# Moving x's rows and the rope tables' inputs behind more of the first weights, and masking the band by memsets on VectorE

## The reference, cut to what matters

```
h = rms_norm(x, mixer_norm)                      # x: (1, 256, 2048)
qkv = h @ w_qkv                                  # 2048 x 3072: 5 chunks of 512 columns with k and v in one
q, k = rope(rms_norm(q)), rope(rms_norm(k))      # cos and sin of positions * inv_freq
x = x + softmax(window(q k) with sinks) v @ w_o
x = x + (silu(h @ w_gate) * (h @ w_up)) @ w_down
...
# chunk_band_attention, 16 heads of 128:
s = q k^T * 128**-0.5 + bias[head, clip(i - j)]  # keys j of later chunks than i's are not in the band
p = softmax(s);  o = p v
```

## Time and profile before

| | us |
|---|---|
| median of 3 runs (lowest, highest) | 2476.63 (2476.08, 2476.88) |
| the profiled execution's own time | 2477.34 |
| its span | 2475.6 |
| PE busy | 2437.5 (98%) |
| DVE busy | 1734.6 (70%) |
| ACT busy | 1159.6 (47%) |
| mean DMA rate | 234 GB/s |
| granted TensorE clock, mean | 0.995 |

### The profile page before, as it was taken

The page is one execution under the profiler, slowest core; times in us unless marked ns, Lnnn a source line. Parts: engine busy times, 40 slices in busy tenths (PEclk is TensorE's granted clock), DMA queues, the critical chain, the costliest instruction groups (busy, mean ns, idle before and its releaser), DMA issues.

```text
span 2475.6 us, 30363 instructions
## 1 busy us (share of the span) xinstructions
PE 2437.5 (98%) x11143; PEld 1990.0 (80%) x11143; DVE 1734.6 (70%) x2394; ACT 1159.6 (47%) x1547; POOL 44.7 (2%) x64
## 2 busy tenths in 40 slices
PE   8999999999999999999999999999999999999997
PEld 6777888888888888788888888888888778888886
DVE  6785777777777776677678667677676576666655
ACT  5565544434443444544444434444444454455553
POOL 1110000000000000000000000000000000000000
PEclk9999999999999999999999999999999999999999
DMA  7434788888888887477777787777776457776653
GB/s 267 138 120 149 253 287 289 304 292 294 290 285 300 291 291 244 137 229 238 239 230 235 243 261 243 240 229 233 246 227 223 144 182 243 248 234 219 215 189 120
DMA packets 161827, 578.13 MB, mean 234 GB/s; under 512 B 18288, under 2 KB 20592, under 8 KB 161680
## 3 DMA queue, kind: packets, MB, share of 16 engines
q1 hardware_dynamic: 160432, 572.64, 70.3%
q0 software_dynamic: 1104, 3.28, 0.5%
q10 hardware_dynamic: 144, 0.26, 0.0%
HBM read 574.01 MB, written 2.10 MB: 233 GB/s over the span
## 4 chain that ended last, share of the span: by engine, by line
PE 92%; DVE 3%; ACT 2%; issue 1%; DMA 1%; SPq 0%; POOL 0%; DVEq 0%; ACTq 0%
PE PS L928 29%; PE PS L930 29%; PE PS L929 29%; PE PS L562 2%; DVE WL L1874 1%; ACT WH L1285 1%; DMA X<-in_x 0%; ACT SQ L963 0%; DVE AR L1394 0%; PE PS L662 0%; PE PS L635 0%; DMA ZG<-in_crow 0%; PE PS L833 0%; PE PS L758 0%; PE PS L778 0%
## 5 line engine op out<-in xcount | busy, mean ns | idle before, releaser
L1874 DVE TENSOR_TENSOR WL<-W,WH 128x1024 fp32r<-128x1024 f32 x816 | 993.6, 1223 | 563.9 <-ACT WH L1285 560.7
L1285 ACT ACTIVATE WH<-W 128x1024 fp32r<-128x1024 f32 x816 | 859.5, 1060 | 950.0 <-PE PS L930 941.5
L928 PE MATMUL PS<-WH,XTH 128*128 128x512 f32 x2144 | 858.5, 400 | 12.0 <-DVE WL L1874 4.7
L930 PE MATMUL PS<-WH,XTL 128*128 128x512 f32 x2144 | 838.3, 391 | 0.0
L929 PE MATMUL PS<-WL,XTH 128*128 128x512 f32 x2144 | 837.0, 390 | 0.0
L928 PEld LDWEIGHTS PS<-WH,XTH 128*128 128x128 f32 x2144 | 403.6, 188 | 103.5 <-issue 18.3
L930 PEld LDWEIGHTS PS<-WH,XTL 128*128 128x128 f32 x2144 | 403.5, 188 | 86.1
L929 PEld LDWEIGHTS PS<-WL,XTH 128*128 128x128 f32 x2144 | 404.1, 188 | 83.1 <-issue 3.8
L928 PE MATMUL PS<-WH,YTH 128*128 128x512 f32 x1120 | 442.1, 395 | 7.6 <-DVE YTL L1407 4.4
L930 PE MATMUL PS<-WH,YTL 128*128 128x512 f32 x1120 | 436.9, 390 | 0.0
L929 PE MATMUL PS<-WL,YTH 128*128 128x512 f32 x1120 | 436.6, 390 | 0.0
(11 more groups left out here) (267 smaller groups left out, 1161.8 us busy)
## 6 DMA issues: line engine op xcount, KB each, us to landing
W<-in_vec SPq DMA_DIRECT2D x192, 512.0 KB, 4.5
W<-in_avoz SPq DMA_DIRECT2D x192, 512.0 KB, 4.5
W<-in_wg SPq DMA_DIRECT2D x88, 512.0 KB, 4.6
W<-in_wu SPq DMA_DIRECT2D x88, 512.0 KB, 4.7
W<-in_wd SPq DMA_DIRECT2D x88, 512.0 KB, 4.7
W<-in_gate SPq DMA_DIRECT2D x64, 512.0 KB, 4.5
W<-in_aqk SPq DMA_DIRECT2D x64, 512.0 KB, 4.7
W<-in_aout SPq DMA_DIRECT2D x64, 512.0 KB, 4.4
```

What stands on the lines that cost most here:

```text
L928: e.matmul(p, x, WH[:, g % NH, j], start=first, stop=False)
L930: i = e.matmul(p, y, WH[:, g % NH, j], start=False, stop=last)
L1285: e.activation(WH[:, n % NH], W[:, i % NW], ACT.Copy).then_inc(s_hi, 1)
L1874: e.tensor_tensor(l, src, h.bitcast(F32), ALU.subtract).then_inc(s_lo, 1)
```

## The change

Five edits. (1) `square_in(0)` stays at the end of chunk 1, `square_in(1)` to `(3)` move to after slots 9, 11 and 12, and `stats(0)` from after slot 9 to after slot 13; X's pieces are issued ahead of tiles 10 to 17 and no longer 6 to 13. (2) Rows, positions and columns are issued after tile 4 and no longer after tile 1, and `rotary` starts one slot later. (3) `kv` is spread to fit (ticks counted from slot 8, two a slot): DVE reaches the factor's wait at tick 13 and no longer 6, `KD` is made at ticks 15 and 17 (9 and 13 before), PE transposes it at ticks 17 and 19 (12 and 14 before), ACT copies at 18 and 20. (4) The first rope of q waits for `s_kd` 2, DVE's own `KD`, and no longer for PE's transposes of it. (5) The mask matmul and `mband` go; DVE writes -1e30 into two blocks of 64 x 64 of the scaled scores with two memsets, and then waits for them before the maximum.

```diff
-    after[1].append(("start", "rotary"))
-    after[7] = [("square_in", 3)]
-    for c, k in enumerate((3, 5, 6)):
-        after[k].append(("square_in", c))
+    after[2].append(("start", "rotary"))
+    after[7] = [("square_in", 0)]
...
-        yield from chunk("X", 0, after={1: [("stats", 0)]} if g == 0 else {})
+        yield from chunk("X", 0, after={1: [("square_in", 1)], 3: [("square_in", 2)], 4: [("square_in", 3)],
+                                             5: [("stats", 0)]} if g == 0 else {})
...
             def kv(par, g):                       # PE
-                yield from ticks(11)
+                yield from ticks(16)
...
-                    e.matmul(b[:, 0:384], idb[:], mband[:], start=True, stop=False)
-                    e.matmul(b[:, 0:128], Q4[:, hh, 0:128], KT[:, h, 0:128], start=False, stop=False)
+                    e.matmul(b[:, 0:128], Q4[:, hh, 0:128], KT[:, h, 0:128], start=True, stop=False)
...
-                yield from ticks(8)               # ACT kv
+                yield from ticks(13)
...
-                yield                             # DVE kv
+                yield from ticks(8)
                 w.wait_ge(s_rst, 1)
...
-                yield from ticks(3)
+                yield from ticks(2)
...
-                    yield from ticks(4)
+                    yield from ticks(2)
...
-                        w.wait_ge(*filled(("kd", 1)))
+                        w.wait_ge(s_kd, 2)
...
                     w.wait_ge(s_bs, n + 1)
+                    for c in (64, 320):
+                        step(e.memset(s[0:64, c:c + 64], NEG))
+                    settle()
...
-            for c in (0, 256):                    # POOL
-                e.memset(mband[0:64, c + 64:c + 128], NEG).then_inc(s_const, 1)
...
-                if NW <= i < NW + 8:              # SP
-                    q = i - NW
+                if 10 <= i < 18:
+                    q = i - 10
...
-                if i == 1:
+                if i == 4:
                     e.dma_start(rows, A["rows"].to_broadcast([128, NROW])).then_inc(s_rows, 16)
                     e.dma_start(posi, A["pos"]).then_inc(s_pos, 16)
                     e.dma_start(cols[:, 32:NCOL], A["cols"][:, 32:NCOL]).then_inc(s_cols, 16)
```

More of the change, by code:

```diff
@@ L343 @@
 NORM_R = {0: 0, 1: 1, 2: 2, 3: 4}
-N_CONST = 13
+N_CONST = 10
 TWO_PI = 2.0 * np.pi
@@ L386, in build @@
         mrow = sb("mrow", [128, 256], BF16)
-        mband = sb("mband", [128, 384], BF16)
         mcT = sb("mcT", [128, 128], BF16)
@@ L1291, in scalar_program @@
             e.dma_start(xs(0), A["xt"][0]).then_inc(s_x[0], 16)
-            w.wait_ge(s_const, 6)
+            w.wait_ge(s_const, 5)
             e.activation(spare, nhalf[:, 0:4], ACT.Copy).then_inc(s_sc, 1)
@@ L1951, in gpsimd_program @@
             w = Waits(e)
-            for t, v in ((ident[:], 0.0), (onesf, 1.0), (mrow[:], 0.0), (mband[:], 0.0), (mcT[:], 0.0),
+            for t, v in ((ident[:], 0.0), (onesf, 1.0), (mrow[:], 0.0), (mcT[:], 0.0),
                          (nhalf[:], -0.5)):
                 e.memset(t, v).then_inc(s_const, 1)
-            w.wait_ge(s_const, 6)
+            w.wait_ge(s_const, 5)
             def select(ap, op, fill, pattern, cm):
@@ L1964, in gpsimd_program @@
             select(mcT[:], ALU.is_ge, NEG, [[1, 128]], -1).then_inc(s_const, 1)
-            for c in (0, 256):
-                e.memset(mband[0:64, c + 64:c + 128], NEG).then_inc(s_const, 1)
-            w.wait_ge(s_const, 12)
+            w.wait_ge(s_const, 9)
             e.tensor_copy(idb[:], ident[:]).then_inc(s_const, 1)
```

## The result

The changed kernel takes 2464.94 us (median of 5 runs, 2463.60 to 2465.74), the kernel before 2476.63 (5 runs, 2474.74 to 2478.77): ratio 0.9954, 95% interval 0.9943 to 0.9964, 11.7 us less. Measured again (run c3) it took 2466.05 against 2475.65, ratio 0.9959 (0.9947 to 0.9972), 9.6 us less.

The account below looks back on a forecast made before the run. PE was taken as the bound nearly everywhere, with much idle time only in the first stage. Terms: 8.1 + 1.7 + 2.7 - 0.5 = 12.0 us saved, forecast median 2464.6 us, range 2462.0 to 2469.5.

Parts of the forecast that it names:

- The start: Slots 2 to 8: slot 8 begins at 33.4 and not 41.54, 8.1 us saved, plus 1.7 from the slow stretch.
- The slow stretch of slots 8 and 9: At the start: half-clock matmuls after 2.38 us idle would go, since that gap goes, 1.7 us saved.
- The 2.65 us for the second tables: On DVE before slot 6: time from the second tables' start to the XTL behind them, taken from the earlier trace.
- kv: Spreading kv makes WL of slot 19 late on DVE, so PE waits: 0.5 us lost, bounds 0 and 2.5.
- the slower rival: Attention: DVE enters q's ropes over some 2 us later, WL late in four groups, 16.4 us lost, 2481 us; 3%.
- the sign of being wrong that I had set: Attention: PE idle beyond 2 us between 66 and 130 us would show the prediction wrong.
- The band: Band, 2190 to 2400 us: PE loses 16 mask matmuls of 0.17 us, 2.7 us saved, between 1.1 and 2.9.
- It costs nothing: Band: DVE's memsets and wait, 0.33 us a head, hide in its 36.5 us idle; without that cover 5.3 us.
- its own sign: Band: PE waiting there would show the prediction wrong; PE idle in the band was to stay 0.
- the lower row that I used: Band: POOL's rows of the same 64 x 64 block, 0.142 us, stood in for each memset of DVE.
- Half clock: Start or attention: a remaining gap or second late WL brings a paid slow stretch; saving 8 to 10.5, 2467.5 us; 20%.
- the central 12.0: Whole kernel: the likeliest saving, 12.0 us, giving a median of 2464.6 us; 62% for 2463 to 2466.5.

Follow-up runs that it names:

- c3: The changed kernel again, unaltered, beside the others on one chip: 2466.05 us.
- b1: The changed kernel with X's pieces issued ahead of tiles 6 to 13 again, squares left late: 2464.75 us, one execution.
- b2: The changed kernel with the tables as before: inputs issued after tile 1, rotary started after slot 1: 2464.20 us, one execution.
- a4: The changed kernel with rows, positions and columns issued after tile 1 again, rotary still one slot later: 2465.11 us, one execution.
- c2: The changed kernel with the tables' inputs issued after tile 3 and not 4: 2462.56 us, one execution.
- b4: The changed kernel with each of ACT's sines taken one tick later: 2462.80 us, one execution.
- b3: The changed kernel with the first rope of q waiting for PE's transposes of the second KD again: 2467.89 us, one execution.
- a3: The changed kernel without the memsets and the wait behind them, so the band is not masked: 2463.73 us, one execution.
- a1: The changed kernel with the mask matmul, mband and constants put back and the memsets taken out: 2466.74 us, ratio 0.9964 to the kernel before.

## Why the prediction was right, point by point

**The start, 9.8 us forecast, 10.1 measured.** The chain worked out for slots 2 to 8 was met slot by slot: 13.2, 15.9, 20.75, 23.5, 27.75, 30.65 and 33.4 forecast, 13.37, 16.09, 20.45, 23.28, 27.52, 30.36 and 33.18 measured. The columns landed at 15.9 (16.1), DVE stood 2.18 us (2.1). The gap before slot 4 is shown as 1.49 and not 2.1: slot 3 ended 0.2 us later than worked out and slot 4 began 0.3 earlier, and the profile counts from a matmul's modelled end (18.97), 0.16 later than the next could have started. The slow stretch of slots 8 and 9 went (1.7 us). b1 confirms the cause named, engines standing at squares. (One rate was misworked: 768 KB per 2.72 us is 282 KB per us and not 290; nothing hangs on it.)

**What it hid.** I priced the start's two edits as one sum and so credited the tables' move with a share. b2 and a4 show that it is worth 0.1 us in all, a gain of 0.8 and a loss of 0.7. That the next late thing was the tables' inputs I had worked out, and c2 shows that it was this change's own doing. The 2.65 us for the second tables I had taken whole from the earlier trace rows; 1.20 of it is DVE's idle time behind ACT's XTH, and b4 takes it away. The number was right and the wait inside it unnamed.

**kv, 0.5 us lost forecast, none measured.** From slot 10 to slot 19 it is 26.06 us before and 25.99 after. With T the start of slot 16 (54.94), WL of slot 19 was done where I had it (T + 9.5), but PE was through with slot 18 only at T + 9.60 and began slot 19 at T + 9.67, since a set of transposes costs it 0.47 us (58.13 - 54.94, less 2.72) and not 0.36; and the kernel before lost 0.15 us there too (from 74.61 to 74.76). The mechanism stands, as b3 shows: 1.6 us more on DVE is 1.6 us on PE. That also moves the slower rival. I put its decision at 2 us of lateness against the kernel before. DVE's first product of the rope comes at T + 2.7 before, at T + 3.6 in the changed kernel (0.9 later, as forecast) and at T + 5.2 in b3 (2.5 later). Lateness past the 0.9 is paid at once, but only once and not in each of four groups: b3 is far from that rival's 16.4 us. The profile shows PE 2.4 us idle from 66 to 130, past the sign of being wrong that I had set (2 us); but the program has moved by 10 us, and over the same work, 55.85 to 119.85, it is 0.95, as before.

**The band, 2.7 us forecast, 2.3 measured.** The step that failed is "It costs nothing", and its own sign, PE waiting in the band, did come (0.2 us, once). Taking the matmul away gives 0.15 to 0.20 us a head, 2.85 in all, more than 16 x 0.17; the memsets cost 0.5 of it (a3). I had looked at DVE's idle time before its splits, and the wait appeared elsewhere, in ACT's order between exponential and copy, after three heads' lateness had added up. The pair of memsets takes 0.19 us, each 0.112, and with the wait behind them the maximum comes 0.26 us later (0.33 taken):

```profile
L1785 DVE MEMSET AR<- x32: 112/112/112, 2189.2 to 2371.4; 64x64 f32 x32
```

That is below the lower row that I used (0.142). By the page "VectorE: DVE Perf Modes" of the Trainium skill, section "Zero memsets can be issued as uint32 (trn2)", it would have been 0.07, an estimate. The second of a pair starts 0.08 us after the first, near to that; the row itself is 0.04 us longer than the estimate.

**Half clock, a rival with 20%.** Neither gap at the start draws a stretch in the two profiles of the changed kernel, and where one came (slot 4 of a1 and a3) it was free, as worked out. But one fell in the attention, 1.5 us, which I had not put on the list. With it the profiled execution comes to 10.1 + 2.3 - 1.5 = 10.9. Another 1.1 lies between slots 139 and 141, where the profile of before takes 7.08 us, the changed one 6.02 and the eleven others 6.02 to 6.54; that is no effect of the change. Small pieces take back 0.4, which gives the 11.6 between the two spans; without a stretch in the attention it would be about 13. So the central 12.0 came out close partly by luck, since these errors cancel: kv +0.5, start +0.3, slots 139 to 141 +1.1, band -0.4, clock -1.5. The second measurement, 9.6 us, is 2.4 off.

## What to carry to other kernels

With engines that execute in order, ask where an engine stands still and what is queued behind it, before asking what the bytes cost: moving the wait gave 8 us, moving X's bytes nothing that can be seen. A wait taken away shows the next one; its time can be worked out slot by slot, and then mended at once (here three small DMAs one tile earlier and ACT's sines one tick later, another 3 us). An idle share of an engine is no proof that added work is hidden: follow the one chain that passes through it, on to the engine that hands over last, and over several rounds, for lateness too small to show in one can add up.

## What the runs showed of the hardware

The clock's fall isn't fixed by the gap alone. After 3.34 and 2.38 us idle a stretch at 1.2 GHz (granted clock 0.50) followed in the profile of before. Before slot 4 it followed 1.91 us in a1 and 1.88 in a3, and did not follow 2.10 in b3, nor 1.49 (after) and 1.65 (b4). Further on, two gaps have the same length in all 13 profiles: 2.20 us before slot 336, with a stretch in 11 of them, and 3.10 before slot 656, with one in 12. In slot 42 of the attention PE has the same three short waits in all 13 profiles (0.8, 0.4 and 0.3 us), and a stretch came behind them in 4. A stretch costs 1.5 to 1.7 us at slot 8 and in the attention, so single executions of one kernel differ by that much, and a median of five can still move by 1 us (2464.94 and 2466.05 for the same kernel). Reading slot starts in a profile told effects of 0.5 us apart that the times could not.
